# Scores of both heads of a pair issued next to each other in the first block's attentions

## The reference, cut to what matters

```python
z = einsum('bhqd,bhkd->bhqk', q[:, :, t0:t1], k[:, :, :t1]) * scale   # the scores
# sb: w = exp(log_sigmoid(z) + excl), excl from a reversed cumulative sum of log_sigmoid(-z)
# mb, fx, ds: p = softmax(z + bias or decay, masked)
out = einsum('bhqk,bhkd->bhqd', p, v[:, :, :t1])
```

## Time and profile before

| | |
|---|---|
| median of 3 runs | 3155.11 us (3155.0 to 3155.15) |
| profiled execution, its own time | 3154.45 us |
| its span, first to last instruction | 3153.1 us |
| mean granted clock of PE | 0.993 of 2.4 GHz |
| busy: PE, DVE, ACT, POOL | 97%, 48%, 23%, 70% |

### The profile page before, as it was taken

One profiled execution on the slowest core, in us unless ns is written; L12 is line 12 of the kernel. 1 busy time (PEld: TensorE's weight loads), 2 busy tenths in 40 slices (PEclk: granted clock), 3 DMA queues, 4 the chain that ended last, 5 costly groups with the idle time before them and its releaser, 6 DMA issues.

```text
span 3153.1 us, 38236 instructions
## 1 busy us (share of the span) xinstructions
PE 3073.2 (97%) x14642; PEld 2486.1 (79%) x14642; DVE 1501.1 (48%) x2248; ACT 711.0 (23%) x1338; POOL 2211.1 (70%) x2524
## 2 busy tenths in 40 slices
PE   8999999999999999998899999999999998999998
PEld 6776777888888888886688888788888876888886
DVE  5367655777247421586643322533224866433214
ACT  3332222222121110333411101211002334211103
POOL 5565667999788877653487877777777443877775
PEclk9999999999999999999999999999999999999999
DMA  4221223333333333321133333333333111333332
GB/s 150 70 71 58 67 74 90 98 94 100 97 95 106 96 98 96 85 56 38 48 101 98 96 105 95 88 94 100 94 100 94 48 53 41 90 98 100 101 98 83
DMA packets 469054, 272.83 MB, mean 87 GB/s; under 512 B 20782, under 2 KB 465120, under 8 KB 468872
## 3 DMA queue, kind: packets, MB, share of 16 engines
q1 hardware_dynamic: 467816, 268.27, 28.8%
q10 hardware_dynamic: 1056, 2.12, 0.2%
HBM read 268.21 MB, written 2.12 MB: 86 GB/s over the span
## 4 chain that ended last, share of the span: by engine, by line
PE 82%; DVE 6%; ACT 1%; POOL 1%; issue 1%; DVEq 0%; POOLq 0%
PE bank L707 16%; PE bank L708 16%; PE bank L712 16%; PE bank L1218 6%; PE bank L1212 6%; PE bank L1213 6%; DVE arena L2215 2%; PE bank L1372 1%; PE bank L741 1%; PE bank L742 1%; PE bank L743 1%; PE bank L800 1%; PE bank L801 1%; POOL wl L672 1%; DVE arena L2224 1%; PE bank L806 1%
## 5 line engine op out<-in xcount | busy, mean ns | idle before, releaser
L672 POOL TENSOR_TENSOR wl<-raw,wh 128x256 fp32r<-128x256 f32 x2016 | 1659.2, 854 | 42.1
L667 POOL TENSOR_SCALAR wh<-raw 128x1024 fp32r<-128x1024 f32 x504 | 553.2, 1098 | 878.3 <-PE bank L712 359.7
L707 PE MATMUL bank<-xh,wh 128*128 128x512 f32 x1552 | 611.1, 394 | 0.5 <-POOL wh L667 0.5
L708 PE MATMUL bank<-xl,wh 128*128 128x512 f32 x1552 | 604.5, 389 | 0.0
L2215 DVE TENSOR_TENSOR arena<-arena 128x512 f32<-128x512 f32 (+2 forms) x485 | 419.2, 881 | 63.3 <-ACT arena L1948 10.4
L2215 DVE TENSOR_TENSOR arena<-bank,nrm 128x512 f32<-128x512 f32 x236 | 152.3, 685 | 512.4 <-PE bank L712 512.0
L712 PE MATMUL bank<-xh,wl 128*128 128x512 f32 x1552 | 386.4, 389 | 0.6 <-POOL wl L672 0.6
L707 PEld LDWEIGHTS bank<-xh,wh 128*128 128x128 f32 x1552 | 291.6, 188 | 71.2 <-issue 5.1
L712 PEld LDWEIGHTS bank<-xh,wl 128*128 128x128 f32 x1552 | 291.2, 188 | 61.4 <-POOL wl L672 1.0
L708 PEld LDWEIGHTS bank<-xl,wh 128*128 128x128 f32 x1552 | 291.4, 188 | 60.5 <-issue 1.2
L707 PE MATMUL bank<-arena_rounded,wh 128*128 128x512 f32 x824 | 322.0, 391 | 1.8 <-DVE arena L2215 1.8
(11 more groups left out here) (357 smaller groups left out, 4214.8 us busy)
## 6 DMA issues: line engine op xcount, KB each, us to landing
raw<-in_ffn_w_gate SPq DMA_DIRECT2D x176, 256.0 KB, 3.1
raw<-in_ffn_w_up SPq DMA_DIRECT2D x176, 256.0 KB, 3.1
raw<-in_ffn_w_down SPq DMA_DIRECT2D x176, 256.0 KB, 2.9
raw<-in_w_in SPq DMA_DIRECT2D x158, 256.0 KB, 3.1
raw<-in_w_up SPq DMA_DIRECT2D x88, 256.0 KB, 3.0
raw<-in_w_gate SPq DMA_DIRECT2D x64, 256.0 KB, 2.9
raw<-in_w_out SPq DMA_DIRECT2D x48, 256.0 KB, 2.9
raw<-in_w_down SPq DMA_DIRECT2D x44, 256.0 KB, 2.9
```

The source lines that it names most:

```text
L667: pool.tensor_scalar(wh[:, s, :], raw[:, s, :], 1.0, 0.0, ALU.mult, ALU.add).then_inc(split, 1)
L672: ins = pool.tensor_tensor(wl[:, s, c], raw[:, s, c], wh[:, s, c].bitcast(F32), ALU.subtract)
L707: pe.matmul(psum, cols(wh, i), xhi, start=(i == 0), stop=False)
L708: pe.matmul(psum, cols(wh, i), xlo, start=False, stop=False)
```

## The change

In PE's program the scores of the first block's attentions are issued by pair. `attentions` gets queries, keys and mask of each branch instead of a score function; `scores(v)` (v even) waits until both banks are free, issues `qk` of both heads one after the other, then the diagonals. sb, which had its own loop, runs through `attentions` too. In it `between(v)` now stands ahead of `scores(v + 2)`, and those are issued at even v. `attention` stays for the second stack's layers. The programs of the other engines aren't changed.

```diff
-        def attentions(runs, between, begun):
+        def attentions(runs, between, start):
             n = NH * TT
             def scores(v):
-                tag, score, _ = runs[v // n]
+                tag, queries, keys, mask, _ = runs[v // n]
                 u = v % n
-                if v >= 2:
-                    pe.wait_ge(*T.at("score_used", runs[(v - 2) // n][0], (v - 2) % n))
-                score(SC[v % 2], *head_block(u)).then_inc(*T.up("score", tag, u))
-            scores(0)
-            scores(1)
-            begun()
+                hh, i = head_block(u)
+                for a in range(2):
+                    if v >= 2:
+                        pe.wait_ge(*T.at("score_used", runs[(v - 2) // n][0], (v - 2 + a) % n))
+                first = qk(SC[0], heads(queries, hh), keys(hh), i, mask is not None)
+                second = qk(SC[1], heads(queries, hh + 1), keys(hh + 1), i, mask is not None)
+                if mask:
+                    first = diagonal(SC[0], i, mask)
+                    second = diagonal(SC[1], i, mask)
+                first.then_inc(*T.up("score", tag, u))
+                second.then_inc(*T.up("score", tag, u + 1))
+            start(lambda: scores(0))
...
                 ins.then_inc(*T.up("turned", tag, u))
-                if v + 2 < len(runs) * n:
+                between(v)
+                if v % 2 == 0 and v + 2 < len(runs) * n:
                     scores(v + 2)
-                between(v)
...
-        attention("sb", score_sb, lambda hh, j: sbv[:, j, hh * HD:hh * HD + HD], 1,
-                  lambda u: behind(SB_BEHIND, (), u), around=values_around)
+        attentions((("sb", sbq, lambda hh: heads(sbk, hh), "strict", lambda hh, j: sbv[:, j, hh * HD:hh * HD + HD]),),
+                   lambda u: behind(SB_BEHIND, (), u), values_around)
...
+        attentions((("mb", mbq, lambda hh: heads(mbk, hh), None, lambda hh, j: mbv[:, j, hh * HD:hh * HD + HD]),
+                    ("fx", fxq, lambda hh: heads(fxk, hh), "causal", lambda hh, j: fxv[:, j, hh * HD:hh * HD + HD]),
+                    ("ds", dsq, lambda hh: dsk[hh % 2 * HD:hh % 2 * HD + HD, :], None, lambda hh, j: dsv[:, j, 0:HD])),
+                   later, scores_first)
```

More of the change, by code:

```diff
@@ L867, in pair_values, with attention @@
             return ins
-        def attention(tag, score, value, mode, between=None, begun=None, behind=None, around=None):
+        def attention(tag, score, value, between, begun, behind):
             def scores(u):
@@ L876, in scores @@
                 score(SC[u % 2], hh, i).then_inc(*T.up("score", tag, u))
-            def first_scores():
-                scores(0)
-                scores(1)
[L882 to L886, removed]
-                begun()
+            scores(0)
+            scores(1)
+            begun()
             for u in range(NH * TT):
@@ L892, in attention @@
                     pe.wait_ge(*T.at("probT", tag, u - 1))
-                p = (prob if mode == 1 else lprob)[:, u % 2, :]
+                p = lprob[:, u % 2, :]
                 for j in range(i + 1):
@@ L898, in attention @@
                     scores(u + 2)
-                if between:
-                    between(u)
+                between(u)
                 if u % 2:
                     pe.wait_ge(*T.at("probT", tag, u))
-                    pair_values(u, value, probT if mode == 1 else lprobT).then_inc(*T.up("pv", tag, u))
-                if behind:
-                    behind(u)
-        def attentions(runs, between, begun):
+                    pair_values(u, value, lprobT).then_inc(*T.up("pv", tag, u))
+                behind(u)
+        def attentions(runs, between, start):
             n = NH * TT
             def scores(v):
-                tag, score, _ = runs[v // n]
+                tag, queries, keys, mask, _ = runs[v // n]
                 u = v % n
-                if v >= 2:
-                    pe.wait_ge(*T.at("score_used", runs[(v - 2) // n][0], (v - 2) % n))
-                score(SC[v % 2], *head_block(u)).then_inc(*T.up("score", tag, u))
-            scores(0)
-            scores(1)
-            begun()
+                hh, i = head_block(u)
[10 more added lines that the diff above has]
+            start(lambda: scores(0))
             for v in range(len(runs) * n):
-                tag, _, value = runs[v // n]
+                tag, _, _, _, value = runs[v // n]
                 u = v % n
@@ L1069, in qk @@
                              stop=not more)
[L1071 to L1085, removed]
         def values_around(first_scores):
@@ L1174, in later, with scores_first @@
                 gate_or_branch(*BEHIND[v])
-        attentions((("mb", score_mb, lambda hh, j: mbv[:, j, hh * HD:hh * HD + HD]),
-                    ("fx", score_fx, lambda hh, j: fxv[:, j, hh * HD:hh * HD + HD]),
-                    ("ds", score_ds, lambda hh, j: dsv[:, j, 0:HD])), later, lambda: gate_or_branch(*AHEAD[1]))
+        def scores_first(first_scores):
+            first_scores()
+            gate_or_branch(*AHEAD[1])
+        attentions((("mb", mbq, lambda hh: heads(mbk, hh), None, lambda hh, j: mbv[:, j, hh * HD:hh * HD + HD]),
+                    ("fx", fxq, lambda hh: heads(fxk, hh), "causal", lambda hh, j: fxv[:, j, hh * HD:hh * HD + HD]),
+                    ("ds", dsq, lambda hh: dsk[hh % 2 * HD:hh % 2 * HD + HD, :], None, lambda hh, j: dsv[:, j, 0:HD])),
+                   later, scores_first)
         for what in LAST:
@@ L1553, in _ @@
             pe.wait_ge(*T.at("k_rot", l))
-            attention(f"ml{l}", score_mla, lambda hh, j: mv[j // 2][:, j % 2, hh * HD:hh * HD + HD], 2, between,
+            attention(f"ml{l}", score_mla, lambda hh, j: mv[j // 2][:, j % 2, hh * HD:hh * HD + HD], between,
                       recurrence_ends, behind_values)
```

## The result

The changed kernel takes 3173.0 us (3169.24 to 3174.13), the kernel before 3155.06 us: a ratio of 1.0058, 95% interval 1.0046 to 1.0070. It is 18 us slower. I had forecast 3159.5 us with a range of 3149 to 3170; I had held "the same within 0.2%" for likelier (0.52) than slower (0.37), and the time lies 3 us outside the range.

What follows compares the result with a forecast made beforehand. PE was taken to bound the first block's attentions. From 3155.1 us, 27.7 saved, 14.5 lost in sb, 12.6 in mb, fx and ds and 5.1 by the clock gave 3159.6, stated as 3159.5; range 3149 to 3170.

Steps and rivals of the forecast that it cites:

- My own sign of being wrong: Would refute the forecast: no PE waits in sb, or more than five half-clock stretches in the profile after.
- What bounds the kernel: First block's attentions: PE is busy almost throughout, so each microsecond it saves is won and each added wait lost.
- Part 1, the pairing: All four branches: two heads' scores overlap and cost one; 5.9 us per branch, 23.1 us saved in all.
- Part 2, tile shapes: Score pairs in all branches: fewer changes to the half-array shape save 0.17 us for each of 27 pairs, 4.6 us.
- Part 3, sb: Branch sb: PE waits seven times for ACT's exp behind the next score's activations; 14.3 us, 14.5 with step 13.
- Part 3, mb, fx and ds: Later branches: DVE loses its lead where the work between is short, so PE waits; 12.6 us together.
- (a): Blocks 10 to 15 of mb, fx, ds: little work between, so PE waits 5.1 us more than before.
- (c): Blocks 7, 19, 21 to 22 and 29: waits at a table, two branches or nothing between; 4.5 us.
- Part 4, the clock: Waits of 2.4 to 2.9 us: three 3.4 us stretches at 1.2 GHz, 1.7 us lost each, 5.1 us.
- R2: Rival: clock falls at nearly every wait; 3175 us, or 3165 with six falls; chance 0.14 with the milder form.
- R5: Rival: some mb, fx, ds waits twice as long since DVE's lead isn't won back; 10 us more, 3169; chance 0.09.
- The row of 2.06 us: Earlier trace, wait until 1451.96: no half clock in the 19 us behind it, taken as evidence against frequent clock falls.

Runs made afterwards that it cites:

- serial: Changed kernel, but in sb and fx each head's diagonal stands between the two scores, so they are no longer adjacent; 3178.6 us.
- evac_first: Changed kernel, but in mb, fx and ds DVE does the gate times branch product ahead of the top-k rounds; 3159.8 us.
- filled: Changed kernel, but PE runs idle transposes of the identity in fourteen of its waits; 3162.8 us.
- after_no_search: Changed kernel without the 48 rounds of top-k search on DVE, every key of ds counting as selected; 3159.2 us.

## Why the prediction was wrong

My own sign of being wrong came, if narrowly: six half-clock stretches, where more than five were to speak against the forecast. The seven waits in sb came as announced (13.1 us, 1.5 to 2.4 each).

*What bounds the kernel:* right. PE does, and its waits showed in the time.

*Part 1, the pairing:* right in price. Pairs take 0.42, 0.63, 0.85 and 1.06 us. But it was booked in full where a wait follows at once: `serial` shows that in sb some 5.5 us of it are no gain. That didn't spoil the sum, since the waits were priced behind a pair that takes as long as one score.

*Part 2, tile shapes:* right in sign, 0.17 taken. Four transposes ahead of a gemm take 0.41 us now, both those behind the values and those behind a pair (0.36 behind a diagonal); with a score next they took 0.59 and 0.53 in the trace before (the earlier trace rows has the 0.53). The gemm ahead of a pair is 0.08 longer. 0.22 us per pair, 5.9 us for 27.

*Part 3, sb:* right. 14.3 us forecast; the seven waits, start to start and less the second diagonal, are 1.7, 2.1, 2.5, 1.7, 1.7, 2.1 and 2.5 us. The 0.2 us booked for step 13 didn't show.

*Part 3, mb, fx and ds:* the first step that failed. 12.6 us of waits were forecast, about 19.6 came (9.8 + 6.2 + 2.1 + 1.5). Right were unit 45 (2.5 us idle, 3.0 forecast with the pipeline's tail) and, in place though not in size, that around unit 29 (1.5 and 0.7 us, 1.3 forecast). Unit 15 waits 2.4 us, where (a) had 5.1: the chain's lateness was mostly paid earlier, at the gemms of units 8 and 12 (2.3 and 3.2 us). What (a) and (c) lacked is the banks. I followed only the chain score, peak, exp, shares, copy; DVE's product behind the search also frees the slab for the next gemm but one, and its margin at unit 8 was 0.4 us. All four of the L707 waits (8, 12, 20 and 36) are for such a product. `evac_first` removes 6.0 us of them by moving the product alone.

*Part 4, the clock:* the second. Three stretches at 1.7 us, 5.1 us, were taken; six came, three of them 6.8 us long, and cost 11.6 us by the rows and 10 by `filled`. I had counted one 3.4 us stretch for each of four waits at the border, and had not priced waits following each other: from 284.1 to 287.2 and from 330.6 to 333.8 PE stands for 3.2 us, with only some 1.2 us of work between that and a first wait of 0.4 to 0.5 us at the values.

*The sum redone:* won 23.1 + 5.9 = 29.0; lost 14.3 in sb, 19.6 in the rest, 11.6 by the clock = 45.5; net 16.5 of the measured 17.9. The stages give 11.2 us more in sb and 7.7 in the rest, 18.8 together.

*The rivals:* R2's mechanism came in a mild form, R5 (longer waits, DVE's lead not won back) too, and each had been held for unlikely alone at 0.14 and 0.09. They aren't independent: with more and longer waits the clock has more occasions to fall, so the range should have held both at once. The row of 2.06 us was no safe border: here waits of 1.94 us were followed by half clock too, and the trace before had a wait of 2.53 us (until 1473.65) with 3.4 us at half clock from 1474.6, which the earlier trace rows left out. The kernel that the Trainium skill describes ("TensorE: Matmul & The Clock Gate", HAM oscillation), cited with R2, waits some 3 to 5 us between its bursts; no wait here is that long but for the 3.2 us at units 12 and 20, so it could not decide for or against R2.

## What to carry to other kernels

When a change moves an instruction behind the work that covered it, list every engine's queue between that instruction and each thing that PE waits for, bank releases included; a margin of 0.4 us appears in no list of the bound engine's waits. Where two units share an issue, each waits for the later of two resources, so a pair costs lead on either side of the covering work; try both places unit by unit and reorder the consumers first. In a PE-bound stage price a wait of about 2 us and more with what the clock may take behind it, here 11.6 us for 22 us of such waits.

## What the runs showed of the hardware

Two float32 scores of 64 rows each, in two instructions each, from the two row halves, run fully side by side: 0.63 us for 256 columns, 1.06 for 512, as one.

The granted clock fell at waits that I had held harmless, and not at each of the same length. In the changed kernel a wait of 1.94 us at 82.3 left it at 2.4 GHz, one of 1.94 at 145.1 was followed by 1.2 GHz from 147.9; one of 2.37 at 98.8 was not followed, one of 2.37 at 162.4 was; and in `after_no_search` a wait of 2.37 us at the same place (u = 4) has half clock from 101.4 us. Nor does the fall wait for the end of a wait: at unit 12 PE went idle at 284.1 and the half clock starts at 284.4, while at 147.9 PE had been busy again for 0.9 us. So it can't be told from a wait's length in this region whether it comes; keeping PE busy with idle transposes avoided it every time from 60 to 495 us and won 10 us.
